# Expert weights copied from the ring into six buffers before TensorE reads them, and heavy experts placed in bit-reversed order

## What is computed

```python
def moe_ffn(h, w_router, b_router, w_gu, b_gu, w_down, b_down):
    logits = (hf @ w_router) + b_router                 # 512 x 32
    top_val, top_idx = lax.top_k(logits, TOP_K)         # 4 experts a token
    gates = jax.nn.softmax(top_val, axis=-1)
    ...
    gu = xb @ w_gu[e] + b_gu[e]                         # 1024 -> 2048
    gt = jnp.minimum(gu[:, :D_FF], SWIGLU_LIMIT)
    up = jnp.clip(gu[:, D_FF:], -SWIGLU_LIMIT, SWIGLU_LIMIT)
    act = (up + 1) * (gt * jax.nn.sigmoid(SWIGLU_ALPHA * gt))
    out = act @ w_down[e] + b_down[e]                   # 1024 -> 1024
    y = y.at[tok].add(out * gate)
```

## Time and profile before

| | us |
|---|---|
| median of 3 executions | 1600.04 (1597.53 to 1602.76) |
| the profiled execution, device time | 1598.5 |
| its span, first to last instruction | 1596.4 |
| blocks begin | 316.0 |
| last matmul ends | 1565.9 |

### The profile page before, as it was taken

One profiled execution on the slowest core, in us unless ns is written; L12 is line 12 of the kernel. 1 busy time (PEld: TensorE's weight loads), 2 busy tenths in 40 slices (PEclk: granted clock), 3 DMA queues, 4 the chain that ended last, 5 costly groups with the idle time before them and its releaser, 6 DMA issues.

```text
span 1596.4 us, 20707 instructions
## 1 busy us (share of the span) xinstructions
PE 1363.0 (85%) x6259; PEld 531.8 (33%) x6260; DVE 473.3 (30%) x1083; ACT 320.4 (20%) x539; POOL 227.1 (14%) x156
## 2 busy tenths in 40 slices
PE   4798998499999999989898989998987777777772
PEld 2586467333233232323232323232322222222220
DVE  3998697621211112121111112121211111111114
ACT  3434541211112111111111111111111111111112
POOL 1740253101011110101010101101010000010001
PEclk9799989799999999999999999999999999999996
DMA  9757024639529669898989999898999999999994
GB/s 375 239 185 261 16 106 154 230 128 383 175 54 386 228 234 381 296 383 298 378 303 357 321 336 341 317 367 302 378 380 385 384 379 382 383 380 379 380 385 156
DMA packets 207171, 474.33 MB, mean 297 GB/s; under 512 B 18482, under 2 KB 18994, under 8 KB 206130
## 3 DMA queue, kind: packets, MB, share of 16 engines
q1 hardware_dynamic: 196322, 455.23, 77.0%
q0 software_dynamic: 10832, 18.90, 5.7%
HBM read 463.05 MB, written 18.35 MB: 302 GB/s over the span
## 4 chain that ended last, share of the span: by engine, by line
PE 36%; SPq 29%; DMA 19%; DVE 9%; issue 5%; ACT 1%; POOL 0%; POOLq 0%; DVEq 0%
SPq L312 23%; PE ps L1398 17%; DMA ring<-in_w_down 10%; PE ps L1410 10%; DMA ring<-in_w_gate_up 6%; SPq L315 4%; DVE bc L822 3%; DMA wm<-in_w_mod 2%; PE ps L1387 1%; PE ps L1273 1%; PE ps L1420 1%; PE ps L1376 1%; PE ps L1297 1%; PE ps L1299 1%; PE ps L1298 1%
## 5 line engine op out<-in xcount | busy, mean ns | idle before, releaser
L1398 PE MATMUL ps<-ring,xT 128*64 128x512 f32 x2880 | 668.3, 606 | 114.4 <-DMA ring<-in_w_gate_up 114.3
L1398 PEld LDWEIGHTS ps<-ring,xT 128*64 128x64 f32 x2880 | 191.4, 137 | 517.7 <-issue 312.1
L1410 PE MATMUL ps<-ring,aT 128*64 128x512 f32 x1440 | 346.1, 605 | 17.1 <-DMA ring<-in_w_down 16.2
L1104 DVE TENSOR_SCALAR gb<-ps 128x256 f32<-128x256 f32 x90 | 38.2, 424 | 974.2 <-PE ps L1398 974.2
L528 POOL DMA_INDIRECT y_rows<-osb,idx_c x46 | 72.3, 1572 | 743.1 <-ACT osb L711 721.9
L1410 PEld LDWEIGHTS ps<-ring,aT 128*64 128x64 f32 x1440 | 88.9, 136 | 178.2 <-issue 122.2
L715 ACT ACTIVATE sg<-gb 128x256 f32<-128x256 f32 x90 | 37.5, 416 | 546.0 <-DVE gb L1104 546.0
L515 POOL DMA_INDIRECT xg<-h_rows,idx_n x46 | 45.2, 982 | 426.4 <-DVE idx_n L998 426.4
L708 ACT ACTIVATE aT<-ps 128x256 f32<-128x256 f32 x90 | 34.5, 383 | 309.1 <-PE ps L1420 293.4
L711 ACT ACTIVATE osb<-ps,gate_c 128x512 f32<-128x512 f32 x46 | 31.6, 687 | 140.4 <-PE ps L1410 139.8
L726 ACT ACT_TABLE_LOAD x45 | 57.7, 1283 | 0.8
(11 more groups left out here) (275 smaller groups left out, 1102.9 us busy)
## 6 DMA issues: line engine op xcount, KB each, us to landing
ring<-in_w_gate_up SPq DMA_DIRECT2D x512, 512.0 KB, 11.8
ring<-in_w_down SPq DMA_DIRECT2D x128, 1024.0 KB, 15.8
wm<-in_w_mod SPq DMA_DIRECT2D x4, 2048.0 KB, 21.8
wm_a<-in_w_mod SPq DMA_DIRECT2D x4, 2048.0 KB, 9.2
wm_b<-in_w_mod SPq DMA_DIRECT2D x4, 2048.0 KB, 8.7
win<-in_w_in SPq DMA_DIRECT2D x3, 2048.0 KB, 20.0
x_in<-in_x SPq DMA_DIRECT2D x1, 2048.0 KB, 10.7
wo_f<-in_w_out SPq DMA_DIRECT2D x1, 2048.0 KB, 7.4
```

The lines of the kernel that those rows point to most:

```text
L1398: last = MMUL(ps[M * j:M * (j + 1), h, :].rearrange("m (g n) -> m g n", g=2), xT[:, k, :], ring[:, c, k % CK, :, j * GW:(j + 1) * GW], sta ...
L1410: last = MMUL(ps[M * y:M * (y + 1), 2, :], aT[:, h, i, M * j:M * (j + 1)], ring[:, c, k % CK, y, :], start=False, stop=(h == 1 and k == 3))
```

## The change

Six buffers `window_0` to `window_5` of 8 KB a partition each are added, and TensorE reads chunk c from `window[c % 6]`. VectorE copies chunks 0 to 5, 8 and 9, ScalarE copies 6, 7, 10 and 11, once for every block, also for the second block of the same expert. A copy waits for the landing of the chunk and for TensorE's use of the chunk six earlier. SyncE's queue waits for the last block's copy in place of TensorE's use. The places of the experts become the bit-reversed ranks. The row numbers (`pick_tokens`) are prepared one block earlier. Other buffers move to make room.

```diff
-    put("not_first", (p > 0)[:, None])
+    put("place", np.array([int(f"{r:05b}"[::-1], 2) for r in [*range(1, NE), 0]])[None])
...
+        window = [at(f"window_{i}", [P, CK, 2, HF], w) for i, w in enumerate((ZD, ZD + 8 * KB, ZD + 16 * KB, ZD + 24 * KB, ZA + 16 * KB, ZB))]
...
+        BY_DVE, BY_ACT = (0, 1, 2, 3, 4, 5, 8, 9), (6, 7, 10, 11)
...
@@ SyncE @@
                 for c in range(NCH):
-                    sp.wait_ge(S["slot_used"], NCH * before + c + 1)
+                    wait_moved(sp, c, before)
...
@@ ScalarE @@
+            def move(c, p, b):
+                act.wait_ge(w_ld[c], landed_at(c) * p + landed_at(c))
+                act.wait_ge(S["slot_used"], NCH * b + c - NW + 1)
+                act.nop(nofuse=True)
+                A(window[c % NW][:, :, :, :], ring[:, c, :, :, :], ACT.Copy).then_inc(S["moved_by_act"], 1)
...
+                    move(6, p, b)
+                    move(7, p, b)
                     sigmoid(0, b)
                     copy_aT(0, b)
+                    move(10, p, b)
+                    move(11, p, b)
                     sigmoid(1, b)
                     copy_aT(1, b)
...
@@ VectorE, ahead of the router's work @@
+            for c in range(4):
+                move(c, 0)
...
@@ VectorE, places @@
+            link(V.memset(place[0:1, 0:1], float(NE - 1)))
+            link(V.scalar_tensor_tensor(keys[:, :], const("expert")[0:NE, :], place[:, 0:1], const("place")[0:NE, :], ALU.is_equal, ALU.mult))
+            link(V.tensor_reduce(place[:, 3:4], keys[:, :], AX.X, ALU.add))
...
@@ VectorE, ahead of the loop: pick_tokens(1), then chunks 4 and 5; in the loop @@
-                    dve.wait_ge(S["meta_done"], b + 1)
-                    pick_tokens(b + 1, e)
+                    dve.wait_ge(S["meta_done"], b + 2)
+                    pick_tokens(b + 2, e)
                     swiglu(0, b)
+                    second(8)
+                    second(9)
...
                     numbers(b + 2)
                     swiglu(1, b)
+                    first_of_next(0)
+                    first_of_next(1)
                     dve.wait_ge(S["bias_used"], b + 1)
                     pick_expert(b + 1)
+                    for c in range(2, NW):
+                        first_of_next(c)
...
@@ TensorE @@
                     if k % CK == 0:
-                        landed(c, e)
+                        wait_moved(pe, c, b)
...
-                                    ring[:, c, k % CK, :, j * GW:(j + 1) * GW], start=False, stop=(k == KD - 1))
+                                    window[c % NW][:, k % CK, :, j * GW:(j + 1) * GW], start=False, stop=(k == KD - 1))
```

More of the change, by code:

```diff
@@ L40 @@
 NCH = 12
+NW = 6
 OUT_OF_RANGE = 4096
@@ L57 @@
 for _name, _n in (("ident", P), ("cd", P), ("neg_sd", P), ("ones", P), ("slot", P), ("before", P),
-                  ("expert", NE), ("expert_of_row", CG), ("part", 1), ("index", 1), ("not_first", 1), ("token", 2 * TL)):
+                  ("expert", NE), ("place", NE), ("expert_of_row", CG), ("part", 1), ("index", 1), ("token", 2 * TL)):
     CST[_name] = (_at, _at + _n)
@@ L248, in build @@
         meta = small("meta", [P, TL, NE, 5], BF16)
[L249 to L252, removed]
+        item_e = small("item_e", [P, NI + 2])
+        item_o = small("item_o", [P, NI + 2])
+        item_i = small("item_i", [P, NI + 2], I32)
+        item_p = small("item_p", [P, NI + 1], I32)
         order_i = small("order_i", [P, NE], I32)
@@ L970, in ffn_norm, with move @@
                     V.tensor_tensor(h_sb[:, t, :], h_sb[:, t, :], bc[:, 1, :], ALU.add).then_inc(S["h_ready"], 1)
+            def move(c, p):
+                dve.wait_ge(w_ld[c], landed_at(c) * p + landed_at(c))
+                V.tensor_copy(window[c % NW][:, :, :, :], ring[:, c, :, :, :]).then_inc(S["moved_by_dve"], 1)
             residual(0)
@@ L1111, in swiglu @@
                 V.tensor_tensor(ab[:, :], ub[:, :], sg[:, :], ALU.mult).then_inc(S["act_ready"], 1)
+            dve.wait_ge(S["meta_done"], 1)
+            e = dve.value_load(item_i[0:1, 1:2], min_val=0, max_val=NE - 1)
+            pick_tokens(1, e)
+            for c in range(4, NW):
+                move(c, 0)
             n = dve.value_load(n_items[0:1, 0:1], min_val=NE, max_val=NI)
@@ L1115, in _, with second, first_of_next @@
                 with dve.If(b < n):
-                    e = dve.value_load(item_i[0:1, bass.ds(b + 1, 1)], min_val=0, max_val=NE - 1)
-                    dve.wait_ge(S["meta_done"], b + 1)
-                    pick_tokens(b + 1, e)
+                    e = dve.value_load(item_i[0:1, bass.ds(b + 2, 1)], min_val=0, max_val=NE - 1)
+                    p = dve.value_load(item_p[0:1, bass.ds(b, 1)], min_val=0, max_val=NE - 1)
+                    p_next = dve.value_load(item_p[0:1, bass.ds(b + 1, 1)], min_val=0, max_val=NE - 1)
+                    def second(c):
+                        dve.wait_ge(S["slot_used"], NCH * b + c - NW + 1)
+                        move(c, p)
+                    def first_of_next(c):
+                        dve.wait_ge(S["slot_used"], NCH * b + NW + c + 1)
+                        move(c, p_next)
+                    dve.wait_ge(S["meta_done"], b + 2)
+                    pick_tokens(b + 2, e)
                     swiglu(0, b)
+                    second(8)
+                    second(9)
                     dve.wait_ge(S["scattered"], 16 * b + 32)
@@ L1387, in bias, with gate_up @@
                 return MMUL(ps[:, bank, :], pick[:, :], bias_w[:, bank * CH:(bank + 1) * CH], start=True, stop=False)
-            def landed(c, e):
-                pe.wait_ge(w_ld[c], landed_at(c) * e + landed_at(c))
-            def gate_up(h, k0, k1, e):
+            def gate_up(h, k0, k1, b):
                 for k in range(k0, k1):
@@ L1410, in down @@
                         last = MMUL(ps[M * y:M * (y + 1), 2, :], aT[:, h, i, M * j:M * (j + 1)],
-                                    ring[:, c, k % CK, y, :], start=False, stop=(h == 1 and k == 3))
+                                    window[c % NW][:, k % CK, y, :], start=False, stop=(h == 1 and k == 3))
                     if k % CK == CK - 1:
```

53 lines of the change are left out of this document (29 added, 24 removed).

## The result

The changed kernel takes **1583.2 us** (1578.88 to 1584.03), the one before 1600.2 on the same chip: ratio 0.989, 95% interval 0.988 to 0.991. That is 17 us faster, where 8 were forecast. Its profiled execution took 1582.56 us with a span of 1580.7, 15.7 us under that of before. 1583.2 lies under the range that was given.

A forecast was written before the change was run, and what follows sets the result against it. The prediction took pairs of a double and a light expert to be bound by transfers plus a dry gap. Its terms, -8.7 - 4.9 - 2.0 + 7.4 + 0.4 = -7.8 us, gave 1592.2 us, range 1586 to 1609.

The forecast's parts named there:

- (7): Queues: SyncE issues the same 640 chunk loads, POOL as many gathers and scatters; 0 us for the streams.
- (4): End of a gated block: 9.3 us after chunk 11's landing (T), before 1.9; paid once at the loop's end, +7.4 us.
- (1): Opening: the queue's first issue in the loop comes at 336.2 and not at 344.92, -8.7 us.
- (5): Ahead of the loop: VectorE's copies of chunks 0 to 3 cost +0.4 us; six copies after the last block cost nothing.
- (2): Each double: next issue 4.3 us after chunk 11's landing (T) in place of 5.0; -4.9 us over seven.
- (3): Experts with three and four blocks: the issue after their gap comes 1.0 us earlier each, -2.0 us.
- (6): Order of the experts: every heavy expert costs one gap wherever it stands, 0 us.
- Rival A: Slower: VectorE copies run at one word a cycle, 2.29 us for 1.22; sum +8.5, 1608.5 us; chance 0.22.
- B: No change: full-speed blocks grow over 26.3 us and the opening's 8.7 us are lost; 1601 us; chance 0.16.
- D: Much faster: the gap closes and pairs fall to TensorE's 71.8 us; 1555 us; chance 0.06, shared with the order rival.
- C: POOL held up: each indirect DMA waits for a copy, 1593.4 us, or 1610 if it waits 3.1 us; chance 0.06.

The follow-up runs named there:

- e12_gather_early: The changed kernel with VectorE's numbers for the next gather moved ahead of the first sigmoid and the copies of chunks 8 and 9: 1597.42 us, ratio 0.9988.
- e10_both_ahead: The changed kernel with both sigmoids ahead of ScalarE's copies and the gather's numbers ahead of VectorE's copies of chunks 8 and 9: 1541.38 us, ratio 0.9633.

## Why the prediction was wrong

The direction was right, and so was the chain of steps from T to the next issue, but the time lay 3 us under the range because one term was put at nothing. Without it the terms of the table add up to -6.2 us where -7.8 were forecast; that these are so near each other is in part luck, since the errors have both signs.

- **The step that failed is (7), the queues**: "POOL's gathers and scatters are as many", and so the streams were taken to keep their length. They are as many, but (4) itself had moved the gather of a gated block from 17 us to 2 us ahead of T, that is out of the stream into the gap. The prediction followed that gather to TensorE, where it costs, and not to the DMA engines, where it pays. `e12_gather_early` gives that back: 13.2 us of streams and 14 us of time, where the change had won 9.5 us of streams.
- (1) -7.0 for -8.3 with (5): blocks begin 0.8 us later instead of 0.4 (316.77 for 316.0), and the issue follows the end of chunk 0's copy (337.27) by 0.7 us, where 0.1 was taken.
- (2) T + 4.4 for T + 4.3. (3) gave -2.0, and -4.2 was measured. After the change each of its two gaps is 0.9 us shorter than forecast: the issue comes 18.4 us into the block ahead (639.43 to 657.87), forecast 18.6, and that block starts at T + 8.6 and not at T + 9.3. Before the change the gap behind the fourfold was 53.2 us, where (3) has 5.0 + 2 x 23.92 = 52.8.
- (4) T + 8.6 for T + 9.3, since the gather of the triple's first block landed 3.8 us after its issue and not 7.1, and the turn of its rows followed at T + 4.3, when TensorE came to it. Full-speed blocks took 23.9 to 24.7 us, not 25.1; as forecast, this cost nothing.
- The end after the loop was forecast at nothing and took 2.4 us more. (5) had the six copies after the last block fall where VectorE waits. They hold VectorE in the last block until the last matmul has ended, and its 18 empty iterations of the loop, 12.2 us, come only then.
- (6) held: 1.0004 for the order alone.
- Rival A fell with the copies of 1.22 us; B, since the opening kept 7 of its 8.7 us; D asked for chunk 0 to be freed before T, and it is what `e10_both_ahead` comes to, by putting sigmoid and numbers ahead of the copies.
- C fell as a term of the time: the last matmul ends 8.6 us after T, less than the 9.3 us that were forecast without it. The Trainium skill, page "SBUF — State Buffer", section "SBUF: two separate sides", has POOL's descriptors wait for a VectorE f32 copy. The traces agree. In the changed kernel 20 of the 46 scatters ran beside such a copy and took 1.98 us in the mean, the other 26 took 1.59; no gather did. In `e12_gather_early` 30 gathers did, with 2.02 us each, against at most 1.18 for the others. One of them, and the copies beside it, of which the first ends at 826.2 and the gather's instruction 0.1 us behind it:

```profile
824.31 2.02 POOL L527 DMA_INDIRECT xg<-h_rows,idx_n  x1 [8.30 <-DVE idx_n L1028]
...
825.01 2.36 DVE L998 COPY window<-ring 128x2048 f32<-128x2048 f32 x2
```

The runs also show why the chance for a surprise on the good side was put too low: the range was built from unknown prices of the new instructions, all of which were right. None of its ends stood for a change in an old term.

## What to carry to other kernels

When a change moves an instruction that starts a transfer, follow the transfer too, on the DMA engines: put it in the dry gap when the gap can't be closed, and ahead of it when it can. Copies that free a buffer early pay only as far as nothing on the path stands behind them on their engine; here the same copies gave 17 us in the change's order of instructions and 58 in another, in which the gather was earlier too. An even order of heavy and light work was worth 2 us or nothing here while each heavy expert cost a gap of its own, and 5.5 us when the gaps behind doubles were gone. And where a stretch ends with a wait, look at what the waiting engine still has to walk through, branches included.

## What was not expected of the hardware

- A gather of 64 rows that lands in a stream lowers the rate of both queues together from 401 to 254 GB/s for 2 us, some 5 us after its issue, and that of the weights alone from 1.02 to 0.45 MB in 2.5 us. It costs a stream 1.4 us, and a little under half of that is its own 0.26 MB.
- TensorE's reads out of the buffer into which the transfers write don't slow these: 1104.2 us of streams with the reads elsewhere, 1103.1 with them in the same order of experts.
- An indirect DMA's instruction on POOL that meets a VectorE copy of 128 x 2048 f32 ends 0.1 us behind the copy in the case shown. In `e12_gather_early` gathers take 2.02 us then, and 0.98 to 1.18 otherwise.
- After TensorE had waited 2.74 us for rows, its granted clock was 0.50 to 0.62 and 16 matmuls took 5.87 us, against 3.65 us at 1.00.
- An empty iteration of the loop costs VectorE 0.68 us in the changed kernel and 0.53 us in the one before. Eighteen of them are 12.2 us, longer than the loads at the end take.
